# Gated linear attention on Trainium2: outputs with the tokens on the partitions, and the forward and backward state of a head stacked into one product

## The chip, the cores and the metric

The kernel runs on one core of a Trainium2 chip, in one launch. The metric is the device time of an execution in microseconds (us), less is better. A core has TensorE (products and transposes), VectorE, ScalarE, GpSimd, and SyncE, which here does nothing but issue DMAs. The engines run at the same time, each through its own instructions in the order in which they are written, and wait for one another on semaphores.

## What is computed

A trunk of two layers over 2048 tokens of width 1024. The first layer has two branches behind one input projection: gated linear attention (GLA) in both directions, and softmax attention over low-rank queries and keys (MLA). Both are gated, concatenated and projected. The second layer is a gated MLP that mixes tokens. The change lies in the GLA branch:

```python
def gla_scan(q, k, v, g, strict):
    # o_t = sum_{s<=t (or s<t if strict)} (q_t * prod_{r=s+1..t} a_r) . k_s  v_s
    ...
        o = jnp.einsum('bhij,bhjv->bhiv', att, vc) + jnp.einsum('bhid,bhdv->bhiv', qc * jnp.exp(b), state)
        state = jnp.exp(b_last)[..., None] * state + jnp.einsum(
            'bhjd,bhjv->bhdv', kc * jnp.exp(b_last[:, :, None, :] - b), vc)

def gla_branch(q, k, v, a_f, a_b, z, ...):
    ...
    o_f = gla_scan(q, k, v, g_f, False)
    o_b = flip(gla_scan(flip(q), flip(k), flip(v), flip(g_b), True))
    o = rms_norm((o_f + o_b).astype(z.dtype), g_norm).reshape(B, S, GLA_WIDTH)
    return o * jax.nn.silu(z)
```

There are 4 heads, with keys of 64 and values of 128. The norm is over the 128 values of a head and token.

## The kernel before

The kernel is written out by hand, for each engine its own program: no scheduler decides an order. Activations between stages lie in DRAM (`projT`, `cumT`, `gla_a`, `gla_vs`, `mixT`), transposed, the channels on the partitions. The stages that matter here:

- **Projection**, to about 591 us: TensorE multiplies. Beside it SyncE, ScalarE and VectorE make the decays: `gates_*` sum the log decays of a block of 128 tokens (`gtots`, one column for each block) and ScalarE's `gates_totals` (L569) takes their exponential (`gtot`). The backward scan runs here as well, from the last block to the first: `back_turn`, `back_contribution` (L799) and `back_state` keep a state `st` of 64 x 128 for each head, the heads two by two on the halves of the partitions, and store it for each block behind the block's values in `gla_vs`. The attention matrices inside a block of 128 tokens are made by `level_*` and lie in `gla_a`.
- **The main loop**, `main_pe`, `main_dve`, `main_act`, `main_pool` and `main_sp` (L1378 to L1629), 16 steps t, one for each block of 128 tokens: the forward scan, the outputs of both directions, norm and gate. The same loop holds the projections of MLA's queries and keys (`lat_*`, L1074 to L1340), which have nothing to do with GLA: in each step `lat_pe(t, 0)` and `lat_pe(t, 1)` issue products of `cqh, wqh` and others (six passes make one block product), in a pattern that repeats every four steps. VectorE's `lat_dve`, ScalarE's `lat_evict` and `lat_act` and GpSimd's `lat_pool` rotate and evict them, and SyncE loads `cq`, `ck`, `kr` and stores the results to `q_all`.
- **Attention** of MLA, from about 765 us, and all that follows.

One step of the loop, for GLA:

- SyncE (`main_sp`, L1378): `load(t + 4)` fetches decays (`m_fe`, L1350), keys and queries (`m_kq`, L1352), values with the backward states behind them (`m_vs`, L1363) and the attention matrices (`attT`, L1358), four DMAs, then the store of `og` to `mixT` (L1395), the gate `m_z` (L1390), and `lat_*`'s loads and stores (L1104 and L1111 store `nst` and `rst` to `q_all`).
- ScalarE: `main_turned` copies the turned keys, `lat_evict` evicts `nst` (L1198), `rstd` copies the spread scales of the step before to `orr` (L1450), `squares` makes `osq` (L1444), `main_factors` makes the five exponentials of the decays, `m_x` (L1371 to L1375), then `lat_act`, which on one step in four begins with a change of the function table for the Sin (L1179) and on another has four activations on `cq` and its neighbours (L1163 to L1172).
- VectorE (`main_dve`, L1466): `normed` (L1503), `mean` (L1496), `q_states` (L1479: the queries times the decays, for the forward state in one half of `qf` and for the backward in another, and for each head zeros on the 64 partitions that are not its own), `state` (L1489, two instructions), `lat_dve`.
- GpSimd (`main_pool`, L1519): `rstd` (L1528, the power -1/2 of 128 x 4), `k_state` (L1524), `gated` (L1533, times silu(z)), `lat_pool`.
- TensorE (`main_pe`, L1547): `contribution` (L1568), `lat_pe`, `sums` (L1600: squares times ones, one column a head), `outputs` (L1587 to L1589), `turn` (L1557), `spread` (L1606: the scales times the identity, so that each stands on all partitions), `lat_pe`.

The output of a head is made transposed, values on the partitions and tokens along the free axis, from three products into one place:

```python
pe.matmul(o, vals[:, h * DV:(h + 1) * DV], attT[s][:, h, :], start=True, stop=False)
pe.matmul(o, m_st[:, t % 2, h // 2, :], qf[t % 2][:, 0, h, :], start=False, stop=False)
mm = pe.matmul(o, back, qf[t % 2][:, 1, h, :], start=False, stop=True)
```

## Time and profile before

| what | value |
| --- | --- |
| median of 3 runs | 2988.22 us (2984.92 to 2988.59) |
| span of the profiled execution | 2985.8 us |
| main loop | about 600 to 765 us |
| one round of the loop (4 steps) | 40.3 us, 645.0 to 685.3 |
| a step's outputs begin (L1587) | 642.05, 651.61, 662.37, 670.86, 682.38 us (steps 4 to 8) |
| attention's first product | 764.97 us |

The time of the profiled execution is told by its span alone. It is 2.4 us under the median of the runs, and inside their range. A step of the loop is not equally long each time, since `lat_*` gives each of four steps another load; four steps together are, so the text speaks of rounds of four.

In a timeline a row is one instruction, or several alike (x8): the start in us from the start of the span, its duration, the engine, the line of the kernel, the operation, what it writes and reads, the partitions x elements, and in brackets the idle time before it and who ended it. TensorE's float32 products run in passes that overlap, so a row's duration is longer than the time to the next row, and the difference of starts is what a pass costs. A row of SyncE (SPq) is the time that issuing a DMA took, not the transfer.

### The profile page before, as it was taken

How to read it: one execution, taken by the hardware profiler on the slowest of the kernel's cores; microseconds unless marked ns; L12 is line 12 of the kernel's file. 1: busy time of each engine (PE TensorE's matmuls, PEld its weight loads, DVE VectorE, ACT ScalarE, POOL GpSimd, SP SyncE). 2: the span in 40 equal slices, each digit the busy share in tenths (PEclk: the TensorE clock that was granted, in tenths of full speed). 3: DMA queues.
4: the chain of work that ended last, by engine and by line, in shares of the span. 5: the costliest groups of instructions: out<-in, count | busy, mean ns of one | idle time of the engine just before them, and what ended most of it. 6: DMA issues, size and time to landing. Idle time of an engine off the chain costs nothing.

```text
span 2985.8 us, 49006 instructions
## 1 busy us (share of the span) xinstructions
PE 2887.8 (97%) x16164; PEld 2405.8 (81%) x16164; DVE 1600.8 (54%) x2733; ACT 1349.8 (45%) x2410; POOL 1165.6 (39%) x1134
## 2 busy tenths in 40 slices
PE   4999999999999999999999999999998999999998
PEld 3768888788788888887887888878887888888887
DVE  6567777755777777774435222255547555532111
ACT  4652254555455555553236111256556656532111
POOL 0211111257333333332330772177676767623221
PEclk8999999999999999999999999999999999999999
DMA  7243355497221111112652332342335232244231
GB/s 263 72 129 104 104 162 163 159 288 220 81 59 57 56 57 56 57 56 90 210 187 107 140 145 84 102 132 96 107 104 183 99 102 95 95 163 158 95 102 56
DMA packets 285737, 357.66 MB, mean 120 GB/s; under 512 B 20196, under 2 KB 190308, under 8 KB 285063
## 3 DMA queue, kind: packets, MB, share of 16 engines
q1 hardware_dynamic: 282536, 344.43, 35.3%
q0 software_dynamic: 3072, 11.54, 0.9%
q8 instruction: 78, 1.28, 0.2%
q14 instruction: 51, 0.42, 0.0%
HBM read 241.99 MB, written 113.90 MB: 119 GB/s over the span
## 4 chain that ended last, share of the span: by engine, by line
PE 87%; DVE 5%; ACT 3%; issue 2%; DMA 2%; POOL 1%; SPq 1%; DVEq 0%; ACTq 0%; POOLq 0%
PE PS L3013 6%; PE PS L3017 6%; PE PS L3021 6%; PE PS L2372 4%; PE PS L2373 4%; PE PS L2374 4%; PE PS L342 4%; PE PS L344 4%; PE PS L343 4%; PE PS L1793 4%; PE PS L1771 4%; PE PS L2540 3%; PE PS L2542 3%; PE PS L2541 3%; PE PS L1794 2%
## 5 line engine op out<-in xcount | busy, mean ns | idle before, releaser
L342 PE MATMUL PS<-hTh,whi 128*128 128x512 f32 x640 | 257.9, 403 | 1.5 <-DVE hTl L296 1.1
L3013 PE MATMUL PS<-hTh,wc 128*128 128x512 f32 x896 | 244.2, 394 | 9.2 <-DVE zu L2947 5.0
L344 PE MATMUL PS<-hTh,wlo 128*128 128x512 f32 x640 | 250.4, 391 | 0.0
L343 PE MATMUL PS<-hTl,whi 128*128 128x512 f32 x640 | 250.4, 391 | 0.0
L2769 POOL TENSOR_TENSOR wc<-wpr,wc 128x512 fp32r<-128x512 f32 x128 | 176.9, 1382 | 179.5 <-ACT wc L2765 179.5
L1874 ACT ACTIVATE pb__164<-PS,nm,rq 128x512 f32<-128x512 f32 x256 | 197.3, 779 | 103.5 <-DVE nm L1937 103.5
L3017 PE MATMUL PS<-hTh,wc 128*128 128x512 f32 x896 | 240.1, 390 | 0.0
L3021 PE MATMUL PS<-hTl,wc 128*128 128x512 f32 x896 | 239.7, 389 | 0.0
L2372 PE MATMUL PS<-ow_h,of_h 128*128 128x512 f32 x576 | 224.4, 390 | 1.4 <-DVE oy L2323 1.4
L2374 PE MATMUL PS<-ow_h,of_l 128*128 128x512 f32 x576 | 224.1, 389 | 0.0
L2373 PE MATMUL PS<-ow_l,of_h 128*128 128x512 f32 x576 | 224.1, 389 | 0.0
L2319 DVE SCALAR_TENSOR_TENSOR oy<-PS,small,gate 128x1024 f32<-128x1024 f32 x32 | 41.0, 1283 | 329.5 <-POOL small L2294 329.4
L1881 ACT ACTIVATE pt<-PS 128x512 fp32r<-128x512 f32 x256 | 139.5, 597 | 156.3 <-PE PS L1771 156.3
L2540 PE MATMUL PS<-vsh,hTh 128*128 128x512 f32 x512 | 199.8, 390 | 2.0 <-DVE vsl L2490 1.6
L3013 PEld LDWEIGHTS PS<-hTh,wc 128*128 128x128 f32 x896 | 166.1, 189 | 44.1 <-issue 11.6
L2542 PE MATMUL PS<-vsh,hTl 128*128 128x512 f32 x512 | 199.2, 389 | 0.0
L2541 PE MATMUL PS<-vsl,hTh 128*128 128x512 f32 x512 | 199.2, 389 | 0.0
L3017 PEld LDWEIGHTS PS<-hTh,wc 128*128 128x128 f32 x896 | 168.6, 188 | 35.5 <-POOL wc L2769 0.2
L3021 PEld LDWEIGHTS PS<-hTl,wc 128*128 128x128 f32 x896 | 168.1, 188 | 35.4 <-DVE hTl L2713 0.4
L2039 POOL TENSOR_TENSOR diag<-ident,rinv 128x128 f32<-128x128 f32 x64 | 37.9, 592 | 390.4 <-PE PS L1781 285.8
L1793 PE MATMUL PS<-pt,mvh 128*128 128x512 f32 x512 | 186.9, 404 | 1.1 <-DVE pt L1950 1.1
L2286 POOL TENSOR_TENSOR of_l<-of,of_h 128x1024 fp32r<-128x1024 f32 (+1 forms) x24 | 84.5, 3520 | 240.2 <-ACT of_h L2247 240.2
(305 smaller groups left out, 7137.0 us busy)
## 6 DMA issues: line engine op xcount, KB each, us to landing
wpr<-wuz SPq DMA_DIRECT2D x128, 256.0 KB, 3.2
projT<-pev SPq DMA_DIRECT2D x80, 256.0 KB, 2.7
xt<-x SPq DMA_DIRECT2D x8, 2048.0 KB, 8.4
mw<-wmod SPq DMA_DIRECT2D x64, 256.0 KB, 2.8
oxt<-x SPq DMA_DIRECT2D x32, 512.0 KB, 4.7
sg_v<-vev SPq DMA_DIRECT2D x64, 256.0 KB, 2.4
vm<-sg_v SPq DMA_DIRECT2D x32, 512.0 KB, 3.8
sgT<-mT SPq DMA_DIRECT2D x32, 512.0 KB, 3.4
```

The costliest lines, as they stand in the source:

```text
L342: pe.matmul(PS[:, bank, :], w[1][:, s, k, :], hTh[:, k, b], start=(k == 0), stop=False)
L343: pe.matmul(PS[:, bank, :], w[1][:, s, k, :], hTl[:, k, b], start=False, stop=False)
L344: mm = pe.matmul(PS[:, bank, :], w[2][:, s, k, :], hTh[:, k, b], start=False, stop=(k == KD - 1))
L1793: pe.matmul(PS[:, 6, :], vh[:, tok], pt[:, k, :, :].rearrange("p a q -> p (a q)"), start=(k == 0), stop=False)
L2372: pe.matmul(o, w["fh"][:, u, k, :], w["h"][:, k, c], start=(k == 0), stop=False)
L2373: pe.matmul(o, w["fh"][:, u, k, :], w["lo"][:, k, c], start=False, stop=False)
L2374: mm = pe.matmul(o, w["fl"][:, u, k, :], w["h"][:, k, c], start=False, stop=(k == OK[l] - 1))
L2540: pe.matmul(o, hTh[:, k, tok], vsh[:, k, :], start=(k == 0), stop=False)
L2541: pe.matmul(o, hTh[:, k, tok], vsl[:, k, :], start=False, stop=False)
L3013: pe.matmul(o, wc[:, k, 0, kk, :], h_tile(hTh, k, kk), start=(kk == 0 and not onto), stop=False, skip_group_check=onto)
L3017: pe.matmul(o, wc[:, k, 1, kk, :], h_tile(hTh, k, kk), start=False, stop=False, skip_group_check=onto)
L3021: mm = pe.matmul(o, wc[:, k, 0, kk, :], h_tile(hTl, k, kk), start=False, stop=(kk == 3), skip_group_check=onto)
```

## The change

The output of a head now has the tokens on the partitions and the values along the free axis. The attention matrix becomes the stationary operand and the values move. The queries times the decays become one tile with the head's forward part on its own 64 partitions and the backward part on the other 64, and the states lie in the same way (`m_sc`: the forward state on one half, the backward on the other), so one product over 128 partitions does what two did over 64 with zeros. What follows from it:

- SyncE: the decays of the backward direction come in two DMAs of 64 partitions with the halves exchanged, so do the queries (`m_qs`, in addition to those in `m_kq`), and the backward states come in two DMAs of their own (`main_states`, 64 x 256), three steps ahead, once the outputs of step t are made (`s_mo`). `m_vs` holds the values alone. `gates_swap` makes an exchanged copy of the backward totals (`gtotsw`) with two DMAs in the projection stage.
- ScalarE: `gates_totals` in two halves, the second behind `gates_swap`; in the loop `rstd` (one copy) goes, and `normed` (four activations with the scale as a pointer operand, 128 x 128 each, to `onr`) stands behind `main_factors` and ahead of `lat_act`.
- VectorE: `mean` is a reduction of `osq` and the scaling; `gated` takes the transposed outputs, the gain and silu(z) in one instruction; `q_states` is four instructions of 64 x 256 in place of two of 64 x 512, `state` four of 64 x 128 in place of two of 128 x 128. Ahead of the loop two memsets and two copies fill `m_sc[0]`.
- GpSimd: `gated` and the memsets of `qf` go.
- TensorE: `sums`, `spread` and one product of each head go; `turned_out` (four transposes of `onr`) comes.
- The backward contribution is written to the other half of the partitions (L799), and semaphore values follow. MLA's attention begins behind `s_mor` and `s_mgz` in place of `s_mog`.

```diff
@@ projection stage
+        def gates_swap(sp):
+            for e in range(2):
+                sp.dma_start(gtotsw[HALF[e], :, :], gtots[HALF[1 - e], 2:4, :]).then_inc(s_gsw, 16)
...
             act.wait_ge(s_gtot, 2 * NG)
-            act.activation(gtot[:, :, :], gtots[:, :, :], ACT.Exp).then_inc(s_gtot, 1)
+            act.activation(gtot[:, 0:2, :], gtots[:, 0:2, :], ACT.Exp).then_inc(s_gtot, 1)
+            act.wait_ge(s_gsw, E_gsw + 32)
+            act.activation(gtot[:, 2:4, :], gtotsw[:, :, :], ACT.Exp).then_inc(s_gtot, 1)
...
-                r = slice(DK * (h % 2), DK * (h % 2) + DK)
-                mm = pe.matmul(PS[r, 6, (2 + h // 2) * DV:(3 + h // 2) * DV], kfT[:, h * DK:(h + 1) * DK],
+                mm = pe.matmul(PS[HALF[1 - h % 2], 6, (2 + h // 2) * DV:(3 + h // 2) * DV], kfT[:, h * DK:(h + 1) * DK],
@@ main_fk, main_vs, main_states
-            sp.dma_start(m_fe[s].rearrange("p d h c -> p (d h) c"), cumT[0:4, :, tok].rearrange("n p c -> p n c")
-                         ).then_inc(s_ml[s], 16)
+            sp.dma_start(m_fe[s][:, 0], cumT[0:2, :, tok].rearrange("n p c -> p n c")).then_inc(s_ml[s], 16)
+            for e in range(2):
+                sp.dma_start(m_fe[s][HALF[e], 1], cumT[2:4, HALF[1 - e], tok].rearrange("n p c -> p n c")).then_inc(s_ml[s], 16)
             sp.dma_start(m_kq[s].rearrange("p h w c -> p (h w) c"), projT[T_GK:T_GK + 4, :, tok].rearrange("n p c -> p n c")
                          ).then_inc(s_ml[s], 16)
+            for e in range(2):
+                sp.dma_start(m_qs[s][HALF[e], :, :], projT[T_GQ:T_GQ + 3:2, HALF[1 - e], tok].rearrange("n p c -> p n c")
+                             ).then_inc(s_ml[s], 16)
...
-            sp.dma_start(m_vs[t % 4][:, :], gla_vs[t, :, :]).then_inc(s_mla[t % 4], 16)
+            sp.dma_start(m_vs[t % 4][:, :], gla_vs[t, :, 0:GH * DV]).then_inc(s_mla[t % 4], 16)
+        def main_states(sp, t):
+            sp.wait_ge(s_bss[(NT - 1 - t) % 2], 16 * ((NT - 1 - t) // 2 + 1))
+            for e in range(2):
+                sp.dma_start(m_sc[t % 3][HALF[1 - e], e].rearrange("p h v -> p (h v)"), gla_vs[t, HALF[1 - e], GH * DV:]
+                             ).then_inc(s_msl[t % 3], 16)
@@ main_sp
                 if t + 4 < NT:
                     load(t + 4)
+                if t + 3 < NT:
+                    sp.wait_ge(s_mo, t + 1)
+                    main_states(sp, t + 3)
@@ main_act
+            def normed(t):
+                act.wait_ge(s_mrr, 2 * t + 2)
                 if t:
-                    act.wait_ge(s_mog, t)
-                act.activation(orr[:, :], PS[:, n_bank(t), :], ACT.Copy).then_inc(s_mor, 1)
+                    act.wait_ge(s_mrb, t)
+                for h in range(GH):
+                    op = act.activation(onr[:, h * P:(h + 1) * P], PS[:, o_bank(t), h * P:(h + 1) * P], ACT.Identity,
+                                        bias=zero[:, 0:1], scale=ocol[:, t % 2, h:h + 1])
+                op.then_inc(s_mor, 1)
@@ main_dve
+                    r, q = HALF[e], HALF[1 - e]
+                    dve.tensor_tensor(qf[t % 2][r, e], m_kq[s][r, :, 1], m_x[t % 2][r, 0], ALU.mult).then_inc(s_mqf, 1)
+                    dve.tensor_tensor(qf[t % 2][q, e], m_qs[s][q], m_x[t % 2][q, 1], ALU.mult).then_inc(s_mqf, 1)
...
+                dve.tensor_reduce(ocol[:, t % 2, :], osq[:, :].rearrange("p (h c) -> p h c", h=GH), AX, ALU.add).then_inc(s_mss, 1)
@@ main_pe
-                    pe.matmul(o, vals[:, h * DV:(h + 1) * DV], attT[s][:, h, :], start=True, stop=False)
-                    pe.matmul(o, m_st[:, t % 2, h // 2, :], qf[t % 2][:, 0, h, :], start=False, stop=False)
-                    mm = pe.matmul(o, back, qf[t % 2][:, 1, h, :], start=False, stop=True)
+                    pe.matmul(o, attT[s][:, h, :], vals[:, h * DV:(h + 1) * DV], start=True, stop=False)
+                    mm = pe.matmul(o, qf[t % 2][:, h % 2, h // 2, :], m_sc[t % 3][:, h % 2, h // 2, :], start=False, stop=True)
...
+                    mm = pe.transpose(PS[:, n_bank(t), h * P:(h + 1) * P], onr[:, h * P:(h + 1) * P], ident[:, :])
```

SyncE's queue in step 4 of the loop (a name's number tells which of its buffers), before:

```order
L1350 DMA m_fe_95<-cumT 128x4x128
L1352 DMA m_kq_99<-projT 128x4x128
L1363 DMA m_vs_111<-gla_vs 128x768
L1358 DMA attT_103<-gla_a 128x512
L1395 DMA mixT<-og 128x4x128
L1390 DMA m_z_109<-projT 128x4x128
L1104 DMA q_all<-nst 128x512
L1111 DMA q_all<-rst 64x512 x4
```

and with the change:

```order
L1358 DMA m_fe_96<-cumT 128x2x128
L1360 DMA m_fe_96<-cumT 64x2x128 x2
L1361 DMA m_kq_100<-projT 128x4x128
L1364 DMA m_qs_116<-projT 64x2x128 x2
L1374 DMA m_vs_112<-gla_vs 128x512
L1370 DMA attT_104<-gla_a 128x512
L1379 DMA m_sc_126<-gla_vs 64x256 x2
L1412 DMA mixT<-og 128x4x128
L1407 DMA m_z_110<-projT 128x4x128
L1112 DMA q_all<-nst 128x512
L1119 DMA q_all<-rst 64x512 x4
```

Ahead of the stores of `og`, `nst` and `rst` stand ten DMAs in place of four: eight loads of the decays, keys, queries, values and attention matrices, and two of states.

TensorE in one step of the loop, before:

```order
L1568 MATMUL PS<-m_vs_111,m_kT_121 64x128 x4
...
L1600 MATMUL PS<-ones,osq 128x1 x4
L1587 MATMUL PS<-attT_103,m_vs_111 128x128
L1588 MATMUL PS<-qf_124,m_st 128x128
L1589 MATMUL PS<-qf_124,m_vs_111 128x128
...
L1557 MATMUL PS<-ident,m_kf 128x128 x2
L1606 MATMUL PS<-ident,ocol 128x128 x4
```

and with the change:

```order
L1592 MATMUL PS<-m_vs_112,m_kT_128 64x128 x4
...
L1611 MATMUL PS<-m_vs_112,attT_104 128x128
L1612 MATMUL PS<-m_sc_127,qf_131 128x128
...
L1581 MATMUL PS<-ident,m_kf 128x128 x2
...
L1623 MATMUL PS<-ident,onr 128x128 x4
L1592 MATMUL PS<-m_vs_113,m_kT_129 64x128 x4
```

The products with `osq` and `ocol` are gone, and the transposes of `onr` stand at the step's end, behind both of `lat_pe`'s parts, where `spread` stood ahead of the second.

VectorE in the same place of the round, before and then with the change, from the rotation of a block product to the next copy of `cq`:

```order
L1255 TENSOR_TENSOR rst<-PS,cosb 128x512
L1503 SCALAR_TENSOR_TENSOR og<-PS,ggn,orr 128x512
L1496 TENSOR_SCALAR ocol<-PS 128x4
L1479 TENSOR_TENSOR qf_125<-m_kq_100,m_x_116 64x4x128 x2
L1489 SCALAR_TENSOR_TENSOR m_st<-m_st,gtot,PS 128x128 x2
L1207 TENSOR_TENSOR krl<-kr_135,krh 128x512
```

```order
L1263 TENSOR_TENSOR rst<-PS,cosb 128x512
L1524 TENSOR_REDUCE ocol<-osq 128x4
L1526 TENSOR_SCALAR ocol<-ocol 128x4
L1534 SCALAR_TENSOR_TENSOR og<-PS,ggn,m_z_110 128x512
L1506 TENSOR_TENSOR qf_132<-m_kq_101,m_x_121 64x256
L1507 TENSOR_TENSOR qf_132<-m_qs_117,m_x_121 64x256
L1506 TENSOR_TENSOR qf_132<-m_kq_101,m_x_121 64x256
L1507 TENSOR_TENSOR qf_132<-m_qs_117,m_x_121 64x256
L1517 SCALAR_TENSOR_TENSOR m_sc_125<-m_sc_127,gtot,PS 64x128 x4
L1215 TENSOR_TENSOR krl<-kr_142,krh 128x512
```

`mean` moved ahead of the instruction that writes `og`, and that one takes the outputs of the step before from TensorE's transposes.

## Rows read from the trace of the kernel before

**Rows 1.** The page's first part: busy us of each engine, share of the span, instructions

```profile
PE 2887.8 (97%) x16164; PEld 2405.8 (81%) x16164; DVE 1600.8 (54%) x2733; ACT 1349.8 (45%) x2410; POOL 1165.6 (39%) x1134
```

**Rows 2.** One round: stretch, length, then busy us by engine, granted clock, DMA share, GB/s

```profile
645.00:685.30 40.30, 38.67 (x282) 34.28 (x281) 24.70 (x41) 22.29 (x47) 30.47 (x25) 0.96 0.84 261
```

**Rows 3.** TensorE's timeline: start us, us, engine and line, operation, tiles, shapes, count

```profile
647.40 0.66 PE L1568 MATMUL PS<-m_vs,m_kT 128*64 128x128 f32 x8
...
680.08 0.50 PE L1337 MATMUL PS<-cqh,wqh 128*128 128x512 f32 x1
...
681.57 0.95 PE L1600 MATMUL PS<-ones,osq 128*128 128x1 f32 x8
682.38 0.47 PE L1587 MATMUL PS<-attT,m_vs 128*128 128x128 f32 x2
...
685.36 1.06 PE L1606 MATMUL PS<-ident,ocol 128*128 128x128 f32 x8
686.17 0.48 PE L1337 MATMUL PS<-cqh,wqh 128*128 128x512 f32 x1
```

**Rows 4.** VectorE's timeline, steps 7 and 8

```profile
671.11 1.40 DVE L1479 TENSOR_TENSOR qf<-m_kq,m_x 64x512 f32<-64x512 f32 x2
672.55 0.60 DVE L1489 SCALAR_TENSOR_TENSOR m_st<-m_st,gtot,PS 128x128 f32<-128x128 f32 x2
673.07 0.88 DVE L1227 TENSOR_TENSOR kr<-kr,cosb 128x512 f32<-128x512 f32 x1
...
677.17 0.68 DVE L1246 TENSOR_TENSOR rsw<-PS,sinb 128x512 f32<-128x512 f32 x1
...
680.21 0.74 DVE L1503 SCALAR_TENSOR_TENSOR og<-PS,ggn,orr 128x512 f32<-128x512 f32 x1
...
685.39 2.29 DVE L1212 TENSOR_TENSOR cql<-cq,cqh 128x1024 fp32r<-128x1024 f32 x1
```

**Rows 5.** VectorE by line and shape: busy us, mean ns; idle before

```profile
L1932 DVE TENSOR_REDUCE mx<-PS 128x1 f32<-128x512 f32 x256 | 165.1, 682 | 1.2 <-PE PS L1764 0.8
```

**Rows 6.** ScalarE's timeline in the loop

```profile
637.48 0.60 ACT L1198 ACTIVATE nst<-PS 128x512 f32<-128x512 f32 x1 [3.38 <-DMA q_all<-nst]
...
650.55 1.28 ACT L1179 ACT_TABLE_LOAD   x1
...
682.12 1.05 ACT L1172 ACTIVATE cqh<-cq 128x1024 fp32r<-128x1024 f32 x1
```

**Rows 7.** ScalarE's timeline in a later stage: four scalings

```profile
2360.75 1.64 ACT L2888 ACTIVATE vm<-vm,vnm,vrs 128x128 f32<-128x128 f32 x4
```

**Rows 8.** GpSimd's timeline, step 8

```profile
682.80 1.42 POOL L1528 TENSOR_TENSOR ocol<-ocol,negh 128x4 f32<-128x4 f32 x1 [1.12 <-DVE ocol L1496]
```

**Rows 9.** SyncE's queue: start us, us to issue, line, DMA, tile and source, count

```profile
621.65 0.38 SPq L1358 DMA_DIRECT2D attT<-gla_a  x1
625.24 0.37 SPq L1350 DMA_DIRECT2D m_fe<-cumT  x1
...
630.12 0.60 SPq L1104 DMA_DIRECT2D q_all<-nst  x1
...
645.01 0.38 SPq L1350 DMA_DIRECT2D m_fe<-cumT  x1
...
648.75 3.23 SPq L1111 DMA_DIRECT2D q_all<-rst  x4
656.19 0.37 SPq L1350 DMA_DIRECT2D m_fe<-cumT  x1
...
662.84 2.46 SPq L1111 DMA_DIRECT2D q_all<-rst  x4
...
670.33 0.43 SPq L1104 DMA_DIRECT2D q_all<-nst  x1
673.81 0.38 SPq L1350 DMA_DIRECT2D m_fe<-cumT  x1
...
677.62 0.49 SPq L1104 DMA_DIRECT2D q_all<-nst  x1
```

More of the change, by code:

```diff
@@ L483, in emit @@
         s_gst = sem("s_gst")
+        s_gsw, E_gsw = s_const, 48
         NG = 8
@@ L933, in proj_pool @@
                 lat_angle(pool, 0, k)
-            pool.wait_ge(s_pb, 8 + NBLK - 2)
-            for p in range(2):
-                pool.memset(qf[p][:, :, :, :], 0.0).then_inc(s_gm, 1)
         def proj_pe(pe):
@@ L963, in emit @@
         m_z = [at("m_z%d" % s, M0 + o * K, [P, GH, P]) for s, o in enumerate((6, 14, 38, 53))]
-        m_vs = [at("m_vs%d" % s, M0 + (32 + 8 * s) * K, [P, GH * DV + 2 * DV]) for s in range(4)]
+        m_vs = [at("m_vs%d" % s, M0 + (32 + 8 * s) * K, [P, GH * DV]) for s in range(4)]
+        m_qs = [at("m_qs%d" % s, M0 + (34 + 8 * s) * K, [P, 2, P]) for s in range(4)]
         m_x = [at("m_x%d" % p, M0 + (35 + 8 * p) * K, [P, 3, 2, P]) for p in range(2)]
         osq = at("osq", M0 + 22 * K, [P, GH * P])
-        orr = at("orr", M0 + 46 * K, [P, GH * P])
+        onr = at("onr", M0 + 46 * K, [P, GH * P])
         m_kf = at("m_kf", M0 + 51 * K, [P, 2, 2, P])
-        m_st = at("m_st", M0 + 30 * K, [P, 2, 2, DV])
+        m_sc = [at("m_sc%d" % j, M0 + o * K, [P, 2, 2, DV]) for j, o in enumerate((30, 66, 74))]
         m_kT = [at("m_kT%d" % p, M0 + (55 + 8 * p) * K, [P, 2 * P]) for p in range(2)]
         og = at("og", M0 + 59 * K, [P, 2, GH, P])
-        qf = [at("qf%d" % p, M0 + (64 + 8 * p) * K, [P, 2, GH, P]) for p in range(2)]
+        qf = [at("qf%d" % p, M0 + (64 + 8 * p) * K, [P, 2, 2, P]) for p in range(2)]
         ocol = at("ocol", M0 + 196 * K + 160, [P, 2, GH])
@@ L1467, in main_dve @@
             dve.wait_ge(s_pb, 8 + NBLK)
-            dve.memset(m_st[:, 0, :, :], 0.0).then_inc(s_gm, 1)
+            dve.wait_ge(s_bs, 2 * NT)
+            for e in range(2):
+                dve.memset(m_sc[0][HALF[e], e], 0.0).then_inc(s_gm, 1)
+                dve.tensor_copy(m_sc[0][HALF[1 - e], e], st[HALF[1 - e], (NT - 1) % 2, :, :]).then_inc(s_gm, 1)
             dve.tensor_scalar(ggn[:, :], ggn[:, :], float(DK) ** -0.5, None, ALU.mult).then_inc(s_gm, 1)
-            dve.wait_ge(s_gm, 8)
+            dve.wait_ge(s_gm, 9)
             def q_states(t):
@@ L1486, in state, with gated @@
                     dve.wait_ge(s_mo, t)
[L1487 removed]
+                    dve.wait_ge(s_ms, 4 * t)
                 for p in range(2):
[L1489 to L1490 removed]
+                    for e in range(2):
+                        r = HALF[e]
+                        dve.scalar_tensor_tensor(m_sc[(t + 1) % 3][r, e, p, :], m_sc[t % 3][r, e, p, :], gtot[r, p, t:t + 1],
+                                                 PS[r, 7, p * DV:(p + 1) * DV], ALU.mult, ALU.add).then_inc(s_ms, 1)
             def mean(t):
+                dve.wait_ge(s_mos, t + 1)
+                if t >= 2:
+                    dve.wait_ge(s_mor, t - 1)
+                dve.tensor_reduce(ocol[:, t % 2, :], osq[:, :].rearrange("p (h c) -> p h c", h=GH), AX, ALU.add).then_inc(s_mss, 1)
                 dve.wait_ge(s_mss, t + 1)
[L1494 to L1496 removed]
+                dve.tensor_scalar(ocol[:, t % 2, :], ocol[:, t % 2, :], 1.0 / (DK * DV), EPS, ALU.mult, ALU.add
                                   ).then_inc(s_mrr, 1)
[L1499 to L1500 removed]
+            def gated(t):
+                dve.wait_ge(s_mrb, t + 1)
+                dve.wait_ge(s_mzl[t % 4], E_mzl + 16 * (t // 4 + 1))
                 if t >= 2:
                     dve.wait_ge(s_mst[t % 2], 16 * (t // 2))
[L1503 to L1504 removed]
+                dve.scalar_tensor_tensor(og[:, t % 2, :, :].rearrange("p h c -> p (h c)"), PS[:, n_bank(t), :], ggn[:, 0:1],
+                                         m_z[t % 4][:, :, :].rearrange("p h c -> p (h c)"), ALU.mult, ALU.mult).then_inc(s_mgz, 1)
             q_states(0)
@@ L1599, in sums @@
                 for h in range(GH):
-                    mm = pe.matmul(PS[:, n_bank(t), h:h + 1], osq[:, h * P:(h + 1) * P], ones[:, 0:1], start=True, stop=True)
-                mm.then_inc(s_mss, 1)
-            def spread(t):
-                pe.wait_ge(s_mrr, 2 * t + 2)
-                for h in range(GH):
-                    mm = pe.matmul(PS[:, n_bank(t), h * P:(h + 1) * P], ocol[:, t % 2, h:h + 1].broadcast_to([P, P]), ident[:, :],
-                                   start=True, stop=True)
+                    mm = pe.transpose(PS[:, n_bank(t), h * P:(h + 1) * P], onr[:, h * P:(h + 1) * P], ident[:, :])
                 mm.then_inc(s_mrb, 1)
@@ L1614, in main_pe @@
                 lat_pe(pe, t, 0)
-                if t:
-                    sums(t - 1)
                 if t < NT:
```

80 lines of the change are left out of this document (30 added, 50 removed).

## The prediction

> **What bounds the kernel now.** I read the busy shares first: TensorE 97% of the span [rows 1], so a microsecond taken from TensorE counts if nothing takes its place. The change touches one stage, the loop of sixteen steps from 600 to 765 us. It repeats every four steps, in 40.3 us, called a round below: TensorE is busy for 38.67 of them, VectorE 24.7, ScalarE 22.3, GpSimd 30.5, the DMA engines 0.84 of the time [rows 2]. TensorE is the bound there, but with no queue far behind it. Then I read the timelines of TensorE, VectorE, ScalarE and GpSimd for the price of each operation [rows 3 to 8], and last SyncE's, for how much of a round it spends on issuing DMAs [rows 9]. The last two decided.
>
> **TensorE's part.** In a step it issues the sums of squares in 0.81 us (681.57 to 682.38), then 24 passes of products in twelve rows of two and a row of two transposes, 2.98 in all (to 685.36), 0.23 a row, and the spreading of the scales in 0.81 (685.36 to 686.17) [rows 3]. Removed: the sums, the spreading, and one of three products, four such rows, 0.92. Added: four transposes, two rows, 0.46. That is 2.1 us a step, 8.4 a round, 33.6 in sixteen steps. If nothing stood in the way, the profiled 2985.8 us would become 2952. I don't believe that sum, for two reasons.
>
> **First: the chain through VectorE and ScalarE.** The norm leaves TensorE and becomes a chain: squares (ScalarE), reduction and scaling (VectorE), power (GpSimd), four scalings (ScalarE), four transposes. A reduction of 128x512 took 0.68 [rows 5], with the small scaling 0.84. The power took 1.42 [rows 8]. Four 128x128 activations with two pointer operands took 1.64 in another stage [rows 7]. On VectorE two multiplications of q took 1.40 for 64x512 each; four of 64x256 take at least that, and with more fixed part about 1.7. Two state updates took 0.60; four of half the partitions and the same length, 1.2 [rows 4]. The gate's multiplication goes from GpSimd into a VectorE instruction that was there (0.74). So VectorE gets 0.7 + 0.3 + 0.6 = 1.6 us a step more, 24.7 + 6.4 = 31 a round; ScalarE loses a copy of 0.5 a step and gains 1.64.
>
> By busy time all of it fits, but the queues are in order. I follow one round, from the end of product 4 (a block product whose bank VectorE then rotates) over product 7 to the next product 4; such a product takes 1.4, the six passes from 680.08 to 681.57 [rows 3]:
> - To the end of product 7, VectorE alone: rotation 0.7, reduction and scaling 0.84, gate 0.75, q 1.7, states 1.2, the rotary keys to the end of L1246 (673.07 to 677.85) 4.8 [rows 4], product 7 1.4: 11.4 us. The walk gives the same stretch the length that it has before.
> - To rsw's sum in the next step: rotation 0.7, reduction 0.84, power 1.42, scalings 1.64, ScalarE's work on cq, which now stands behind the scalings, 3.0 (four activations, the last of them 682.12 to 683.17) [rows 6], cql 2.3, rsw 0.7 and its sum 0.7 [rows 4]: 11.3. The narrow products (L1321, 2.7 us) wait for rsw.
> - To product 4: reduction 0.84, power 1.42, scalings 1.64, the Sin block with its table load 3.3 (four instructions, the first at 650.55), copies and squares 1.3, a table load 1.3 [rows 6], factors 1.5 (five at 0.3, under the 0.41 of one of the four 128x128 [rows 7], since they overlap), q 1.7, states 1.2, ckv 0.7, product 4 1.4, waits 0.2: 16.5.
> The round is 11.4 + 11.3 + 16.5 = 39.2 against 40.3. Of 8.4 us saved, 1.1 are left, and TensorE idles some 10 us a round. The granted clock is 0.96 in the round now [rows 2], so 3.4 us of it at 1.2 GHz instead of 2.4. What the new gaps of up to 4 us do to it no row tells; between nothing and one more such stretch (3.4 us at half speed, 1.7), I take 0.8. A round is 40.0.
>
> The Trainium skill (TensorE: Matmul & The Clock Gate, Part 4) says that transposes don't count as busy time for the clock as products do. By it I would take 1.7 in place of 0.8, a round of 40.9; no row here separates it.
>
> **Second: SyncE's queue.** The loads and states of a step grow from four DMAs to ten: the decays in three pieces, q's other half in two, the backward states in two; six of the ten have 64 partitions. In a round SyncE issues 44 DMAs now, in bursts from 645.01 to 651.98, 656.19 to 670.76 and 673.81 to 678.11, 25.8 us, 0.59 each [rows 9]. In a burst a DMA costs between 0.42 (one takes 0.38, as at 645.01, and a gap follows) and 0.62 (four of 64 partitions in 2.46) [rows 9]. 24 more cost 10.1 to 14.9, a round of 35.9 to 40.7; at 0.55, nearer to the 64-partition rows that they resemble, 39.0. So 14.5 us of slack are gone. SyncE also enters late. Ahead of the first store of a query block (630.12) [rows 9] stand 28 of the new DMAs, 15.4 us, with one idle stretch of 3.1 to hide them (from 622.03 to 625.24) and up to 2.4 of stalls that a slower queue doesn't meet: it leaves 10 us later. ScalarE's next eviction into that buffer waits for its landing, for 3.38 us even now (637.48) [rows 6], and behind that stand squares, factors and scalings. Today TensorE's step ends 10 us after that eviction (at 647.40) [rows 3]; it can end 5.3 after it (eviction and squares 1.1, reduction 0.8, power 1.4, scalings 1.6, transposes 0.4). So at the end of step 4 TensorE is some 5 us late.
>
> **The sum**, on the profiled execution of 2985.8 us:
> - entry, to the end of step 4: +5.0
> - steps 5 to 12, two rounds of 40.0 in place of 40.3: -0.6
> - the last four steps, by the same walk 35.4 against 36.8 (no loads, no factors at the end): -1.4
> - VectorE's memsets and copies ahead of the first step take 0.8 more, inside what the entry is late anyway: 0; GpSimd's two memsets that go had idle time behind them: 0
> - two DMAs for the swapped totals in the projection stage, where TensorE is the bound and ScalarE half idle: 0, or 1 if the exponential that waits for them holds up an eviction; I take 0
>
> Together +3, less 1 for GpSimd's lighter load (its 1.7 us a step of gate no longer slow VectorE's copies beside it): +2, 2988. The median of the runs is 2.4 above this execution: 2990.
>
> **The rivals.**
> A, slower: SyncE's queue is the bound. At 0.62 a DMA, with the stalls of the entry staying, the first store is 28 x 0.62 - 3.1 = 14.3 late, the end of step 4 9.6; two rounds of 40.7, +0.8; the tail -1.4: +9, 2997. It decides from about 0.57 a DMA up. For it: the 64-partition DMAs are the dearest of the rows. Against it: they may be so because the DMA engines were full then.
> The Trainium skill (DMA: Bandwidth & Descriptors, Rules for kernel authors) says of two transfers to disjoint partition halves "Don't bother", use one of 128, and its SBUF page (SBUF — State Buffer, Door 1) that 64 partitions reach half of the ports. As a mechanism of this kernel it is A with late landings: full engines move 311 GB/s (261 at a share of 0.84), so 384 KB of halves a step at half of that are 1.3 us a step more; the DMA engines' 33.9 us of a round (0.84 of 40.3) become 39.0 [rows 2], under 40, so it doesn't decide alone but puts A at 3000. No row here separates it.
> B: the chain is shorter than walked. cql (2.29) [rows 4] is twice the length of instructions of 0.7 to 0.9, so some of it may be GpSimd's doing, which is lighter now. A round of 37 with DMAs at 0.45: entry +2, three rounds and the tail -13, together -11: 2977, and 2970 if the round falls to 36.5 and the entry is hidden.
> C: TensorE's saving goes through whole: 2952 + 2.4, 2954. It needs slack that the walk does not find.
>
> **How the numbers follow.** A measurement here tells about 0.2%, 6 us, from no change. Forecast 0.46 (2982 to 2996: three quarters of it within 0.2%, most of the rest slower), A 0.22, B 0.25, C 0.07. Faster: 0.02 from the forecast, 0.22 from B, 0.07 from C, 0.31. Slower: 0.10 from the forecast, 0.20 from A, 0.30. The same: 0.39. The range reaches over B and most of A, and leaves out C and the tops: 2970 to 3001.
>
> **What would show it.** Right: TensorE's busy time in the loop falls by about 33 us and its idle time rises by nearly as much; a round is near 40 us; SyncE's queue has next to no idle time in steps 0 to 11, its first query store leaves near 640; ScalarE waits for that store's landing and for GpSimd's power. A round under 38 us with SyncE idle in it would make both reasons wrong. A round above 41, with TensorE waiting for loads, is A. A changed time outside of 590 to 780 us would mean a part that I missed.

## The result

The changed kernel takes 3008.72 us, median of 4 runs (3007.97 to 3013.28), the kernel before beside it 2987.04: a ratio of 1.0076, 95% interval 1.0064 to 1.0089, 22 us slower. The forecast was 2990, the range ended at 3001. The profiled execution has a span of 3006.2 against 2985.8.

Where the products of the outputs of steps 4, 8 and 12 begin, and attention's first product, in us from the start (from TensorE's timelines; e1 and so on are the experiments below, and each median stands beside that of before in its own comparison):

| kernel | step 4 | step 8 | step 12 | attention | median (before) |
| --- | --- | --- | --- | --- | --- |
| before | 642.1 | 682.4 | 722.7 | 765.0 | 2987.0 |
| changed | 654.2 | 701.7 | 747.4 | 789.5 | 3008.7 (2987.0) |
| e1 four loads | 645.8 | 690.1 | 732.8 | 775.3 | 2996.3 (2985.0) |
| e2 before, ten DMAs, halves | 658.1 | 705.2 | 750.7 | 793.0 | 3011.1 (2985.0) |
| e3 before, ten DMAs, whole | 650.0 | 695.8 | 737.7 | 780.0 | 3000.4 (2985.0) |
| e4 copies in DRAM | 647.7 | 692.0 | 734.7 | 777.4 | 2998.2 (2985.0) |
| e5 e4, mean first | 650.7 | 692.1 | 736.2 | 773.8 | 2990.4 (2986.7) |
| e9 changed, store first | 646.6 | 693.3 | 737.5 | 777.0 | 2997.2 (2987.7) |
| e10 e5, store first | 646.9 | 688.3 | 729.4 | 767.4 | 2988.8 (2987.7) |
| e12 all moves | 645.1 | 688.4 | 730.7 | 770.8 | 2986.3 (2987.7) |
| e15 e12 with fillers | 647.2 | 684.8 | 723.1 | 761.7 | 2976.5 (2985.1) |

The outputs of step 4 are 12.2 us late, a round takes 47.5 and then 45.7 in place of 40.3, and attention begins 24.5 late. The span is 20.4 longer. The 4 us between are no gain of the change that can be told: from attention's first product to the next change of ScalarE's function table behind it (1591.5 before, 1613.1 after) the traces take 826.6 and 823.6 us, and the traces of all kernels in this text 822 to 831, those of e8 and e16, which leave the stage as before, 823.4 and 822.8. So one trace tells the loop better than it tells the span, and a median tells the whole. The page's first part and the stretch of one round and of the whole loop, after (columns as in [rows 1] and [rows 2]; the stretches of a round in this text are cut at the load of the stationary operand ahead of the outputs, up to 0.7 us before their first product):

```profile
PE 2872.8 (96%) x15844; PEld 2386.2 (79%) x15844; DVE 1637.1 (54%) x2814; ACT 1363.9 (45%) x2459; POOL 1137.3 (38%) x1116
```

```profile
653.80:701.50 47.70, 36.92 (x202) 30.96 (x201) 33.88 (x61) 25.93 (x59) 23.29 (x21) 0.79 0.77 231
600.00:760.00 160.00, 119.02 (x674) 101.35 (x675) 113.87 (x214) 88.14 (x198) 72.23 (x62) 0.82 0.80 239
```

The same 160 us of the kernel before:

```profile
600.00:760.00 160.00, 153.47 (x1104) 137.18 (x1101) 93.76 (x160) 86.38 (x178) 103.95 (x85) 0.94 0.78 239
```

Over the whole execution TensorE's busy time fell by 15.0 us only (2887.8 [rows 1] to 2872.8), not by 33: the products are gone, but what is left runs at a granted clock of 0.82 in place of 0.94. A round holds 10.8 us without a product on TensorE, where 1.6 were before [rows 2]. The waits between 600 and 790 us (engine, line, what it waited for: us in total, times, longest), after:

```profile
ACT nst L1206 <- DMA q_all<-nst: 41.5, 5, 14.0
ACT onr L1472 <- POOL ocol L1559: 25.7, 12, 6.7
...
PE PS L1345 <- DVE rsw L1254: 14.9, 3, 5.8
...
PE PS L1345 <- DVE ck L1229: 12.6, 4, 4.0
```

and of the kernel before:

```profile
ACT nst L1198 <- DMA q_all<-nst: 9.4, 4, 3.4
```

ScalarE waits 32 us more for stores of `nst` to land. Its line for the eviction ahead of step 8, TensorE's product that waits for such an eviction ahead of step 4, and SyncE's queue (columns as in [rows 9]) at the first such store and in one step of loads:

```profile
698.66 0.60 ACT L1206 ACTIVATE nst<-PS 128x512 f32<-128x512 f32 x1 [9.97 <-DMA q_all<-nst]
```

```profile
651.50 0.80 PE L1345 MATMUL PS<-cqh,wqh 128*128 128x512 f32 x1 [5.12 <-ACT nst L1206]
```

```profile
644.15 0.43 SPq L1112 DMA_DIRECT2D q_all<-nst  x1
...
668.28 0.53 SPq L1358 DMA_DIRECT2D m_fe<-cumT  x1
668.86 1.42 SPq L1360 DMA_DIRECT2D m_fe<-cumT  x2
670.32 0.60 SPq L1361 DMA_DIRECT2D m_kq<-projT  x1
670.96 1.26 SPq L1364 DMA_DIRECT2D m_qs<-projT  x2
672.26 0.59 SPq L1374 DMA_DIRECT2D m_vs<-gla_vs  x1
...
673.42 1.11 SPq L1379 DMA_DIRECT2D m_sc<-gla_vs  x2
```

The first store leaves at 644.15, 14.0 us later than before (630.12 [rows 9]). A pair of halves of decays or queries takes 1.26 to 1.42, 0.63 or more each, a pair of states 1.11, and the whole DMAs of keys and values next to them 0.6. From 657.2 to 702.0 SyncE issues 68 DMAs, 41.9 us of issuing, 0.62 each (0.66 with the gaps). They don't land later for it: from issue to landing in a round (KB each, median us), after and then before:

```profile
m_vs<-gla_vs SPq DMA_DIRECT2D x4, 256.0 KB, 3.0
attT<-gla_a SPq DMA_DIRECT2D x4, 256.0 KB, 3.0
...
m_qs<-projT SPq DMA_DIRECT2D x8, 64.0 KB, 3.2
```

```profile
m_vs<-gla_vs SPq DMA_DIRECT2D x4, 384.0 KB, 4.9
...
attT<-gla_a SPq DMA_DIRECT2D x4, 256.0 KB, 5.7
```

So rival A seems to hold, without the late landings. Its sign, TensorE waiting for loads, shows only once (3.1 us for a state, in step 3): it is ScalarE that waits, for the store, and TensorE for ScalarE. Whether this is all of the 22 us the next runs tell.

### The profile page after: what moved, and what is told of

Read it like the earlier page. It is cut to its first block, busy times and chain, and to the rows that moved or that the text cites. A ratio compares the mean times of both kernels' runs of the same rounds, so it can differ in the third digit from the quotient of the medians.

```text
span 3006.2 us, 48573 instructions
## 1 busy us (share of the span) xinstructions
PE 2872.8 (96%) x15844; PEld 2386.2 (79%) x15844; DVE 1637.1 (54%) x2814; ACT 1363.9 (45%) x2459; POOL 1137.3 (38%) x1116
## 3 DMA queue, kind: packets, MB, share of 16 engines
q8 instruction: 76, 1.25, 0.2%
## 4 chain that ended last, share of the span: by engine, by line
PE 83%; DVE 5%; issue 4%; ACT 3%; DMA 2%; POOL 2%; SPq 1%; DVEq 0%; ACTq 0%; POOLq 0%
PE PS L3024 6%; PE PS L3028 6%; PE PS L3032 6%; PE PS L2383 4%; PE PS L2385 4%; PE PS L2384 4%; PE PS L342 4%; PE PS L344 4%; PE PS L343 4%; PE PS L1804 4%; PE PS L1782 4%; PE PS L2551 4%; PE PS L2552 3%; PE PS L2553 3%; PE PS L1805 2%
```

## The experiments

Gains and losses between kernels of different comparisons are taken from their ratios to the kernel before, 0.1% of which is 3 us. The theories: **Q**, SyncE's queue, as in A. **C**, the chain through the in-order queues of VectorE, ScalarE and GpSimd, later **W** for its one place, the norm behind a rotation. **P**, the halves of the partitions. **G**, TensorE's clock.

### The queue alone and the chain alone: e1 to e4

e1, the changed kernel with the loads of before:

```diff
-            sp.dma_start(m_fe[s][:, 0], cumT[0:2, :, tok].rearrange("n p c -> p n c")).then_inc(s_ml[s], 16)
-            for e in range(2):
-                sp.dma_start(m_fe[s][HALF[e], 1], cumT[2:4, HALF[1 - e], tok].rearrange("n p c -> p n c")).then_inc(s_ml[s], 16)
+            sp.dma_start(m_fe[s].rearrange("p d h c -> p (d h) c"), cumT[0:4, :, tok].rearrange("n p c -> p n c")
...
-            sp.dma_start(m_vs[t % 4][:, :], gla_vs[t, :, 0:GH * DV]).then_inc(s_mla[t % 4], 16)
+            sp.dma_start(m_vs[t % 4][:, :], gla_vs[t, :, :]).then_inc(s_mla[t % 4], 16)
...
-                    main_states(sp, t + 3)
```

> The changed kernel on all engines but SyncE, whose queue is that of before: four loads a step (the decays not exchanged, the backward states behind the values and not used, no exchanged queries, so VectorE multiplies the unexchanged ones and the backward state of steps 1 to 15 is zero). Left out: the right backward part of the outputs. Theory Q (SyncE's queue is the bound, each DMA of a burst some 0.65 us, and ScalarE's evictions of nst wait for stores that leave late): the wait of ScalarE for the stores of nst falls from 41 us to under 10, a round from 47 to 37 to 40 us, the time to 2970 to 2986. Rival C (the in-order chain of VectorE, ScalarE and GpSimd with TensorE's lower clock is the bound, and the queue only happens to be full): a round stays at 44 or more, the time over 3000. Rival P (DMAs of 64 partitions land late): like Q here, since all of them are gone.

Measured: 2996.26, ratio 1.0034 (1.0021 to 1.0047). Neither theory alone: 12 us of the 22 go with the queue, the first round falls from 47.5 to 44.3, but 10 us over the kernel before stay, with a queue that is that of before. ScalarE's wait for the stores is 11.7 us in total here, and its wait for GpSimd's power has grown to 48.2.

e2 and e3, the kernel before with ten DMAs a step:

```diff
+            for e in range(2):
+                sp.dma_start(m_fe[s][HALF[e], 1], cumT[2:4, HALF[e], tok].rearrange("n p c -> p n c")).then_inc(s_ml[s], 16)
```

and in e3 in its place

```diff
+            for e in range(2):
+                sp.dma_start(m_fe[s][:, 1, e], cumT[2 + e, :, tok]).then_inc(s_ml[s], 16)
```

The same is done to keys and queries, and to values and states.

> The kernel before, with ten DMAs a step in place of four: decays in three, keys and queries in three, values and states in three, six of them halves of 64 partitions, same bytes. All other engines as before. Q: SyncE's queue fills here too, 68 DMAs a round at 0.65 are 44 us against 40.3, and the entry is late by some 10: 2998 to 3010. C: no change, 2985 to 2990. P: slower too, as Q.

> As e2, ten DMAs a step and the same bytes, but every one reaches all 128 partitions and the pieces are split along the columns. Q (the number counts): within 3 us of e2. P (the halves count): near before, 2985 to 2992. C: no change from before in both.

Measured: e2 3011.12, ratio 1.0082 (1.0065 to 1.0099). e3 3000.39, ratio 1.0059 (1.0042 to 1.0076). Six more DMAs a step, with nothing else changed, cost the kernel before 24 us as halves and 18 as whole ones. Q expected the two within 3 us of each other and missed: they lie 11 apart (the intervals of the ratios overlap a little; step 4 comes 8.1 us later with halves). SyncE's queue in e2, and then in e3:

```profile
631.74 1.25 SPq L1354 DMA_DIRECT2D m_fe<-cumT  x2
...
646.75 0.43 SPq L1104 DMA_DIRECT2D q_all<-nst  x1
```

```profile
625.83 0.95 SPq L1354 DMA_DIRECT2D m_fe<-cumT  x2
...
638.04 0.43 SPq L1104 DMA_DIRECT2D q_all<-nst  x1
```

A pair of halves costs 1.25, a pair of whole ones with the same bytes 0.95: the number counts, and a half is dearer to issue. The first store leaves 16.6 us late with halves and 7.9 with whole ones. Two transfers to disjoint halves are thus no way to gain anything here, as the Trainium skill has it (DMA: Bandwidth & Descriptors, Rules for kernel authors), but the loss is in the issue: in e2's round from step 4 the halves land after 2.5 to 3.1 us and `attT` after 3.4, where it took 5.7 before. So P is right only as a dearer issue.

One thing in these runs goes beyond the theories. In e2, with all engines but SyncE as before, the rounds take 47.1 and 45.6 us, as long as in the changed kernel (47.5 and 45.7), and the whole costs 24 us, where the change costs 22. So ten DMAs a step alone are enough for such a round, with either chain, and the 24 us of the queue (e2) and the 10 of the chain (e1) don't add up to the change: they overlap.

e4, the changed kernel with exchanged copies written to DRAM in the projection stage:

```diff
+                if n >= 2:
+                    for e in range(2):
+                        sp.dma_start(cumT[n, HALF[e], tb * 512:(tb + 1) * 512], gcum[HALF[1 - e], u, :]).then_inc(s_gst, 16)
...
+            sp.dma_start(m_qs[s][:, :, :], projS[:, :, tok].rearrange("n p c -> p n c")).then_inc(s_ml[s], 16)
```

> The changed kernel with seven DMAs a step: exchanged copies of the backward decays and of the queries are written to DRAM in the projection stage (32 more stores of 64 partitions there, where SyncE has idle time), so that the loop loads the decays in one DMA and the exchanged queries in one. Bytes loaded in the loop are those of the changed kernel. Q: 56 DMAs a round are 36 us, so the queue is no longer the bound; a round is 38 to 41, entry some 3 late: 2980 to 2992. C: as after, over 3000. P: two of the six halves are left, so some 2990 to 2996.

Measured: 2998.18, ratio 1.0050 (1.0033 to 1.0067): 8 us gained, less than Q expected, with rounds like e1's (44.3, 42.7). e1 shows that some 10 us are not the queue. Of e4's 15 over before a part still is, since ScalarE waits 22.3 us for stores of `nst` in it, 9.4 in the kernel before.

### What the chain costs: e5 to e8

The path in e1, round 2, on VectorE, GpSimd and ScalarE:

```profile
686.20 0.69 DVE L1261 TENSOR_TENSOR rst<-PS,cosb 128x512 f32<-128x512 f32 x1 [2.29 <-PE PS L1345]
686.81 0.68 DVE L1517 TENSOR_REDUCE ocol<-osq 128x4 f32<-128x512 f32 x1
```

```profile
687.77 1.04 POOL L1552 TENSOR_TENSOR ocol<-ocol,negh 128x4 f32<-128x4 f32 x1 [5.86 <-DVE ocol L1519]
```

```profile
679.16 0.59 ACT L1456 ACTIVATE osq<-PS 128x512 f32<-128x512 f32 x1
...
688.84 1.50 ACT L1463 ACTIVATE onr<-PS,zero,ocol 128x128 f32<-128x128 f32 x4 [7.63 <-POOL ocol L1552]
690.22 0.64 ACT L1169 ACTIVATE krh<-kr 128x512 fp32r<-128x512 f32 x1
```

The squares are ready at 679.75. Their reduction begins at 686.81, behind a rotation that waits for TensorE's product, which waits for rsw, which stands behind the rotary keys. ScalarE stands still for 7.6 us, with the work on cq behind it.

```diff
                 if 1 <= t <= NT:
                     mean(t - 1)
+                lat_rotate(dve, t - 1)
```

where `lat_rotate` is the last rotation, taken out of `lat_dve(t - 1)` (e5), and on ScalarE (e6):

```diff
-                if 1 <= t <= NT:
+                if 1 <= t <= NT and t % 4:
                     normed(t - 1)
                 lat_act(act, t)
+                if 1 <= t <= NT and t % 4 == 0:
+                    normed(t - 1)
```

> e4 with one thing moved on VectorE: the reduction of the squares and the small scaling stand ahead of the last rotation of the step before (L1261 in e1), which waits for a block product on TensorE, and not behind it. Theory W (what is left over before, 11 to 13 us with four or seven DMAs, is the norm's way through VectorE's queue: in the steps with a rotation GpSimd waits 5 us for the reduction, ScalarE 4 to 8 us for GpSimd, and what stands behind the scalings on ScalarE waits too): steps of 11.9 and 15.5 us lose 1 to 3 each, a round falls from 44.3 to 39 to 42, the time from 2998 to 2984 to 2992. Theory G (TensorE's clock: the round is long because products after gaps of 4 to 5 us run at half speed): the gaps stay, since the product still waits for rsw; gain under 3 us.

> e4 with one thing moved on ScalarE: in every fourth step the four scalings stand behind the activations on cq (krh, sqq, sqk, cqh) and not ahead of them. W: those activations no longer wait 7.6 us for GpSimd, cql and rsw on VectorE come earlier, the 15.5 us steps lose 2 to 4: a round of 41 to 43, the time 2988 to 2995. G: under 3 us gained.

e7 and e8 put rsw and its sum ahead of the rotary keys, in e4 and in the kernel before.

> e4 with one thing moved on VectorE: rsw and its sum stand ahead of the four instructions on the rotary keys and ckl (4.5 us), so that TensorE's block product behind rsw can begin some 4 us earlier and has no gap of 5 us ahead of it. G: the product runs at full speed (1.4 and not 2.7 us), a round loses 3 to 6 us: 2980 to 2990. W: the reduction comes no earlier than the rotary keys end: 0 to 3 us gained in all.

> The kernel before with the same move as e7 (rsw and its sum ahead of the rotary keys): TensorE's gap of 1.63 us ahead of that product goes, four times in the loop, if nothing takes its place: 0 to 6 us faster than before, 2979 to 2986. It tells how much of a gain in e7 belongs to the move and not to the change.

Measured: e5 2990.40, ratio 1.0014 (1.0005 to 1.0024), e6 2994.16 (1.0019 to 1.0044), e7 3000.93 (1.0034 to 1.0070), e8 2984.75 (0.9983 to 1.0002). By the medians, moving one reduction ahead of one rotation is worth 11 us (the ends of the two intervals allow 3 to 18), and in e5 ScalarE's wait for the power in the step with the work on cq is short (0.6 us, 3.5 in e4). Just ahead it still waits for the store of `nst`, 6.9 us (5.7 in e4):

```profile
688.47 0.60 ACT L1220 ACTIVATE nst<-PS 128x512 f32<-128x512 f32 x1 [6.85 <-DMA q_all<-nst]
...
691.64 1.51 ACT L1488 ACTIVATE onr<-PS,zero,ocol 128x128 f32<-128x128 f32 x4 [0.61 <-POOL ocol L1576]
```

From e4 to e5 ScalarE's wait for the power falls from 39.1 us in total to 12.0, the one for stores stays (22.3, 21.8), and 12.3 us of waiting for TensorE's transposes come. In the traces attention begins only 3.6 us earlier in e5 than in e4, and 10.0 earlier in e10 below, where the store goes first as well. W holds, and its full worth shows only with the store out of the way.

e6 gained 6 by the medians, as expected, though its interval overlaps e4's. e7 did nothing alone, so G missed there: the step behind rsw got shorter (from 15.5 to 9.2 us) and the next one longer (from 8.3 to 14.1). e8 is no change that can be told.

### The place of the store, and all moves together: e9 to e12

```diff
             for t in range(NT + 2):
+                if t >= 2:
+                    nope_store(sp, (t - 2) // 4, (t - 2) % 4)
                 if t + 4 < NT:
                     load(t + 4)
```

> The changed kernel, ten DMAs a step as it has, with one thing moved in SyncE's queue: the store of nst stands at the head of a step, ahead of the loads of step t+4, the states, the store of og and the load of the gate, not behind them. Q in its narrow form (what costs is that ScalarE's eviction waits for a store that stands behind ten to twelve DMAs): the 41 us of ScalarE's waits for the stores fall below 15, the time from 3008.7 to 2996 to 3003. Q in its wide form (the number of DMAs times 0.65 us limits the round, wherever the store stands): a round stays at 45 to 47, the time at 3004 to 3010.

Measured: 2997.24, ratio 1.0033 (1.0022 to 1.0045). The changed kernel with its ten DMAs gains 13 us from the place of one store, as much as from taking the DMAs away (e1). Q's narrow form holds for the time. In the traces 7.6 us of it come at the entry, to step 4; the first round is still 46.7 us, as the wide form had it, and the second 44.3. ScalarE's waits, e9:

```profile
ACT onr L1472 <- POOL ocol L1559: 54.4, 13, 7.1
...
ACT nst L1204 <- DMA q_all<-nst: 1.8, 1, 1.8
```

41.5 us of waiting for stores became 1.8, and the wait for the power went from 25.7 to 54.4: under the one lay the other.

e10 is e5 with the store first, e11 is e10 with e7's move, e12 is e11 with e6's.

> e5 (seven DMAs, the reduction ahead of the rotation) with the store of nst at the head of a step in SyncE's queue. In e5 ScalarE still waits up to 6.9 us for that store, which stands behind the store of og, and that one behind GpSimd's and ScalarE's norm. W and Q together: that wait goes, steps of 12 and 13 us lose 1 to 3, 2982 to 2988. If the wait only gives way to another (TensorE waits for rsw and ck at the same time): 2988 to 2991.

> e10 with rsw and its sum ahead of the rotary keys on VectorE as well. With the reduction and the store out of the way TensorE's gap of 4 us ahead of the product behind rsw is what is left in that step: 2976 to 2985 if it goes for good, as e10 if the step is then bound by the reduction behind the rotary keys.

> e11 with the scalings behind the activations on cq in every fourth step (as e6): 0 to 4 us less than e11. If all of the change's saving on TensorE could be had by order alone, 2955 to 2970; if TensorE's clock (0.84 in the loop against 0.94 before) keeps what the gaps cost, 2972 to 2984.

Measured: e10 2988.75, ratio 1.0004 (0.9992 to 1.0017). e11 2990.11 (0.9998 to 1.0018). e12 2986.29, 0.9993 (0.9983 to 1.0002). e10 came out as its second case, in which the wait gives way to another: ScalarE waits 25.5 us for TensorE's transposes in it. e11 missed what was expected of it: with the step behind rsw short, the next is the long one again. e12 is 4 us under e11, and above both of its ranges for what the saving or the clock would allow. All of it brings the changed kernel level with the one before, not below it: the 22 us were queue and order. Its rounds are still 43.3 and 42.3, and attention begins 5.8 us later than before in its trace.

### TensorE's clock: e13 to e16

The product behind rsw, in e1 and in the kernel before, by stretch (length, busy us of the engines, granted clock, DMA share, GB/s):

```profile
683.20:686.00 2.80, 2.76 (x7) 2.11 (x8) 0.69 (x1) 0.00 (x0) 0.00 (x0) 0.50 0.83 291
```

```profile
677.90:679.50 1.60, 1.60 (x7) 1.06 (x8) 1.03 (x1) 1.60 (x5) 1.51 (x2) 1.00 0.98 297
```

The same six passes take 2.7 us at 1.2 GHz after a gap of 5.10 and 1.6 at 2.4 GHz after one of 1.63, and that product lies on the chain. The fillers come with a wait for the turned keys, since these lie in the same bank:

```diff
+                if (n, tb > 0) in WARM:
+                    pe.wait_ge(s_mkT, min(t + 1 + part, NT))
+                for _ in range(WARM.get((n, tb > 0), 0)):
+                    pe.matmul(PS[:, 6, 256:512], wqh[:, 0, 0:P], cqh[:, 0, 0:256], start=True, stop=True)
```

> e4 with small products of no use on TensorE, into a part of a bank that nothing reads, put into its two longest gaps of a round (25 of 256 columns ahead of the product behind ck, 36 ahead of the one behind rsw, about 3 to 4 us each). Theory G (a part of the 12 us is the clock: after a gap of 4 to 5 us the next 3.4 or 6.8 us of products run at 1.2 GHz, of which a product of 1.4 us becomes 2.7 on the chain): the granted clock of the loop rises from 0.85 to above 0.92, a round falls from 44.3 by 2 to 4, the time from 2998 to 2988 to 2994. If products on the chain weren't what the clock cost: no change, or slower by what the fillers overrun.

> e10 with the same fillers (25 ahead of the product behind ck, 16 ahead of the one behind rsw, where the gap is 2 to 3 us). G: 2978 to 2985, faster than before. Otherwise as e10, 2989.

> e12 with fillers ahead of the product behind ck (25) and of the sums of cq (15), its two gaps of a round. G: 2975 to 2983. Otherwise as e12, 2986.

Measured: e13 3006.32, ratio 1.0066 (1.0049 to 1.0083), e14 2982.88, 0.9992 (0.9983 to 1.0001), e15 2976.45, 0.9967 (0.9954 to 0.9979). In e13 the filler did its work on the product, but the time rose by 5 against e4 by the medians (the intervals overlap), where a gain was expected. TensorE's timeline, there and at the last such product, and then the first one's stretch:

```profile
682.17 4.47 PE L1333 MATMUL PS<-cqh,wqh 128*128 128x256 f32 x36
687.69 0.50 PE L1365 MATMUL PS<-cqh,wqh 128*128 128x512 f32 x1 [1.05 <-DVE rsw L1268]
...
772.55 4.47 PE L1333 MATMUL PS<-cqh,wqh 128*128 128x256 f32 x36
```

```profile
687.70:689.20 1.50, 1.50 (x7) 1.19 (x8) 0.66 (x1) 0.00 (x0) 0.00 (x0) 1.00 1.08 351
```

1.5 us in place of 2.8. Half of the loss in e13 lies at the end: outputs of step 15 come 4.2 us later than in e4 and attention 7.9, where e4 had a gap of 0.2 us ahead of the last such product and 36 fillers of 4.5 us don't fit. Of the rest, 2.4 were there at step 4; the first round was shorter than e4's (42.6 for 44.3), the second longer (45.6 for 42.7). Why was not tried by itself. Where the number was fitted to the gaps, the fillers are worth 4 us (e10 to e14, intervals that overlap) and 8 (e12 to e15, which don't). e12 and then e15, a round from step 5 on and the loop:

```profile
658.80:701.30 42.50, 35.05 (x201) 29.95 (x201) 31.99 (x62) 26.24 (x60) 22.42 (x20) 0.82 0.86 260
600.00:760.00 160.00, 131.97 (x826) 113.64 (x826) 120.73 (x240) 99.85 (x227) 77.22 (x72) 0.82 0.84 260
```

```profile
657.40:695.60 38.20, 35.59 (x236) 30.86 (x236) 30.72 (x58) 25.44 (x58) 21.50 (x20) 0.92 0.89 268
600.00:760.00 160.00, 148.42 (x1017) 129.47 (x1018) 126.52 (x249) 102.93 (x231) 78.41 (x75) 0.90 0.85 261
```

Useless products lifted the granted clock from 0.82 to 0.92, and the two rounds from step 4 to step 12 fell from 85.7 to 75.9 us, 4.9 each. The control gives fillers to the kernel before, in its own gap:

> The kernel before with the fillers alone: 10 small products into bank 6 ahead of the product behind rsw, where TensorE has its gap of 1.6 us in every round. It tells whether e15's gain over before belongs to the change or to the fillers. If the kernel before loses nothing to the clock that fillers can bring back (0.94 in the loop): 2983 to 2990, no change. If fillers alone do it: 2974 to 2980, like e15.

Measured: 2985.84, ratio 1.0003 (0.9992 to 1.0014). So e15's 0.33% isn't the fillers' alone. e15 is the one kernel that beats both. Its trace has attention 3.3 us earlier than before; the rest of its 10 us lies behind the loop or in what one trace doesn't tell, and no run located it. What the kernel before would gain from e7's move and the fillers together wasn't tried; with the move alone it is e8, in which TensorE has no gap over 0.6 us in the rounds left to fill, and e15 lies below it too (0.9954 to 0.9979 against 0.9983 to 1.0002).

## Why the prediction was wrong

- **TensorE's part** (2.1 us a step) is right as a sum of removed work. The forecast that it would not come through was right too, and so was each of the two reasons by name. The sizes were not, and all of them erred to the same side.
- **Second reason, the entry.** "At 0.55, nearer to the 64-partition rows that they resemble" is the first step that failed: four of the six halves took 0.63 and two 0.56, and whole DMAs beside them rose (keys and queries from 0.51 to 0.60, values 0.45 to 0.59, `og` 0.42 to 0.58). The store was to leave 10 us late and left 14.0 late. The step after it, that TensorE "can end 5.3 after" the eviction, is the second: it let only the norm stand behind the eviction. TensorE's own product waits for it too (651.50, 5.1 us idle), and behind that product stand the outputs, another product and the transposes, so the step ends 8.3 us behind the eviction (650.85 to 659.15) and 11.8 late in place of "some 5". Of the 12.2 us by which the outputs of step 4 are late the queue has 8.4 and the chain 3.8 (e1).
- **Second reason, the round.** Rival A put a round at 40.7, the larger of the queue's issuing and the chain. The run shows 47.5, with 41.9 us of issuing in it, and so does the kernel before with ten DMAs (e2, 47.1), whose chain is the old one. So neither the time on the queue nor the chain of the forecast is what such a round lasts: the queue acts through what stands behind it, the store that ScalarE's eviction waits for. That it closes into a ring (the next loads wait for the outputs, and these for the eviction) can be read from the program; the runs don't show what share of a round it has, since e9, without the late store, still has 46.7 and 44.3.
- **First reason, the chain.** The walk gave 39.2 for a round, e1 measures 44.0 from one rotation behind product 4 to the next, in the three stretches of the walk 14.25, 10.0 and 19.7 for 11.4, 11.3 and 16.5:

```profile
671.95 0.69 DVE L1261 TENSOR_TENSOR rst<-PS,cosb 128x512 f32<-128x512 f32 x1 [2.42 <-PE PS L1345]
...
696.23 0.68 DVE L1517 TENSOR_REDUCE ocol<-osq 128x4 f32<-128x512 f32 x1
...
715.95 0.69 DVE L1261 TENSOR_TENSOR rst<-PS,cosb 128x512 f32<-128x512 f32 x1 [2.91 <-PE PS L1345]
```

  The first has its end at 686.20, shown above. Two terms were too small, each in the first and in the third stretch: the block product, taken at 1.4 and measured at 2.7 and 2.85, at the lower clock, and the four multiplications of q, 1.7 for 2.4 and 3.1. The states (1.5 for 1.2) and the rotary keys to rsw (5.2 for 4.8) add less, and cql took 1.6 for 2.3, which rival B had suspected. The walk followed the right instructions; what it did not use is that it already showed `mean` behind the rotation, the place where e5 and e10 gained.
- **The clock.** "Between nothing and one more such stretch, I take 0.8" a round. Measured: 0.79 to 0.85 in a round for 0.96, and the lower clock falls on both products on the chain, some 2.7 us a round there alone. Fillers bring 4.9 us a round back. Of the Trainium skill's rule (TensorE: Matmul & The Clock Gate, Part 4), that transposes don't count as busy time, nothing was shown: gaps of 4 to 5 us came ahead of the slow products, and no run varied the transposes alone.
- **The small terms.** The totals' exchange and VectorE's start cost nothing that shows (step 0 begins at 599.8, before 600.2). "Less 1 for GpSimd's lighter load" was not separated. The tail was to give 1.4 back; from step 12 to attention it took 42.2 where 42.3 were before.
- **The rivals.** A was the right one as to what is slower, with 0.22, and its 14.3 for the late store is close to the 14.0 measured. It was too small by 12 us, since it kept the forecast's 5.3 behind the eviction and the forecast's chain, and took a round for the larger of the two. B and C fell.

## What to carry to other kernels

Count DMAs by their time on the issuing queue, at the price of the nearest shape, and look at what stands behind them in that queue: here the place of one store was worth as much as the six DMAs a step. Don't take the larger of the queue's time and the chain's for the round: follow what waits for what the queue sends late (41.9 us of issuing in a round, and the round took 47.5). When work leaves TensorE for a chain through three engines, find the instruction in each in-order queue behind which the chain's link stands, and move that first, together with what it would wait for next (e5, and e10 with the store). Where TensorE then idles, the gaps are paid twice, by the gap and by the slower products behind it, and a forecast must put the slow product on the chain where it stands.
